# A norm's sum of squares: seven of eight blocks added on GpSimd, two products on TensorE

## The chip, the cores and the metric
One core of a Trainium2 chip runs the whole kernel. The metric is the device time in microseconds, the median of three runs: 1757.07 us before (1756.89 to 1757.11).

## The reference, cut to what matters
A decoder trunk of two layers for 288 tokens (256 of a prompt, 32 of eight samples) of width 1024, in float32. The part that the change touches is the norm, which is computed five times:

```python
def rms_norm(x, g):
    y = xf * lax.rsqrt(jnp.mean(xf * xf, axis=-1, keepdims=True) + RMS_EPS)
    return (y * g).astype(x.dtype)
for layer in range(2):
    h = rms_norm(x, g_norm1[layer]) * (1 + scale1) + shift1     # norms 0 and 2
    ...                                                         # input projection, mixer, output projection
    x = x + gate1 * (concat(o_a, o_b) @ w_out[layer])
    h = rms_norm(x, g_norm2[layer]) * (1 + scale2) + shift2     # norms 1 and 3
    f = swiglu(h, ...) if layer == 0 else moe_swiglu(h, ...)    # dense, then 8 experts
    x = x + gate2 * f
return rms_norm(x, g_final)                                     # norm 4
```

The weights are 1 MB units (w_ada for scale, shift and gate; w_in; w_out; the feed-forward weights), of which some 486 MB are read, most of it in the experts' stage.

## The kernel before, in words
Activations lie channel-major: x is 128 partitions by eight blocks of 288 tokens (`x3[:, d]`, d from 0 to 7; `KD` is 8, `T` is 288). So the mean over channels is a sum over partitions and blocks. A norm n does it in three steps. ScalarE squares block after block as soon as x is ready (`squares`, line 718), into `sqx[n]`, and counts `sq_ready`. TensorE multiplies each block by a matrix of ones and adds up the eight products in one PSUM bank (`norm` of the tensor program, lines 1749 to 1757); a product of two float32 operands is two weight loads and two matmul instructions. ScalarE then makes rstd of it by a logarithm and an exponential (lines 710 and 711), and VectorE forms h (`hf`).

Every engine runs its own program in order, and they wait for each other by semaphores. SP loads the 1 MB units into a ring of six raw buffers; a load waits until the unit six places before it has been used. What lies around the norms:

- Norms 1 and 3 stand behind the output projection. TensorE's products (line 1894) are made into x block by block by three VectorE instructions each (`add_gated`, lines 1453, 1454 and 1458; the last adds two SBUF tensors for the samples). Between them VectorE updates the sample states (line 1436), four heads in two halves. GpSimd writes each head's state out when its second half is done (`gdns_out`, line 665).
- Behind norm 1 TensorE runs four pairs of conditioning products (`ada_run`, line 1722, with short products of line 1732 between them), each from two 1 MB units, and then the dense layer. Behind norm 3 come the router and the experts.
- Norm 2 stands behind the down projection, of whose eight blocks one is ready every 8 us or so; behind it TensorE runs four pairs of conditioning products and then the input projection of layer 1. GpSimd meanwhile waits for x of the last block, clears two pads (line 626), loads their sample rows by DMA (lines 628 and 629), and later forms products for a convolution (line 641).
- Norm 0 works on the input, norm 4 on the result. GpSimd's other arithmetic is the masks of a triangular inverse (line 618).

Of the kernel before, what the change touches and what calls it, by code (L numbers as in the profile page):

```python
# [26 lines left out]
F32 = mybir.dt.float32  # L27
# [3 lines left out]
ALU = mybir.AluOpType  # L31
# [5 lines left out]
KD = D // P  # L37
# [3 lines left out]
T = TP + TS  # L41
# [8 lines left out]
NE = 8  # L50
# [111 lines left out]


SCATTER_AT = range(1, 17, 2)
GATED_AT = range(18, 34, 2)
# [101 lines left out]
def program(nc, units, x_in, c_in, par_in, const_in, gdn_in, qst_in, cst_in,  # L267
            y_out, gdnp_out, gdns_out, qst_out, cst_out):
    ctx = ExitStack()
    with ctx:  # L270
# [24 lines left out]
        sg = keep("sg", 2 * T)  # L295
# [102 lines left out]
        def cc(name, rows=P, cols=None):  # L398
            a, b = CCOL[name]
            return con[0:rows, a:(b if cols is None else a + cols)]  # L400

        def kt(t, n=KD):
            return t[:, :].rearrange("p (k t) -> p k t", k=n)
# [8 lines left out]
        def per_token(m9):  # L412
# [18 lines left out]
        cs_ready, cstat_ready, expa_ready = sem("cs_ready"), sem("cstat_ready"), sem("expa_ready")  # L431
        row_ready, modT_ready, mod_ready = sem("row_ready"), sem("modT_ready"), sem("mod_ready")
        x_ready, sq_ready, ss_ready, rstd_ready = sem("x_ready"), sem("sq_ready"), sem("ss_ready"), sem("rstd_ready")
        hf_ready, hhi_ready, hlo_ready = sem("hf_ready"), sem("hhi_ready"), sem("hlo_ready")
        pad_ready, ab_done, ab_copied, conv_done = sem("pad_ready"), sem("ab_done"), sem("ab_copied"), sem("conv_done")
        silu_done = sem("silu_done")
        low_ready = sem("low_ready")
        posm_ready, parts_ready = sem("posm_ready"), sem("parts_ready")
        router_ready, parts_done, parts_copied = sem("router_ready"), sem("parts_done"), sem("parts_copied")
        moe_added = sem("moe_added")  # L440
# [27 lines left out]
            sem(n) for n in ("tokT_done", "tok_hi_ready", "tok_lo_ready", "lg_done", "lsub_ready", "lexp_ready"))  # L468
        sel_ready, pos_done, npass_ready, posT_ready = (
            sem(n) for n in ("sel_ready", "pos_done", "npass_ready", "posT_ready"))  # L470
        psel_ready, gx_done, gx_copied, gt_done, gw_done, hthi_ready, htlo_ready, ptsel_ready = (
# [135 lines left out]
        def _(pool):  # L607
# [3 lines left out]
            def level_mask(l, b, blk_i, n, q, s):  # L611
# [6 lines left out]
                pool.tensor_tensor(heads(blk[b]["MT"], n, n), heads(blk[b]["AT"], n, n), mask, ALU.mult).then_inc(mt_ready, 1)  # L618

            pool.wait_ge(par_loaded, 16)  # L620
            pool.wait_ge(masks_loaded, 16)
            for l in range(DEPTH):
                if l:
                    pool.wait_ge(st_out, 64 * l)
                    pool.wait_ge(x_ready, 2 * KD * l)
# [37 lines left out]
                for h in range(H):  # L663
                    pool.wait_ge(sst_ready, H * l + h + 1)
                    pool.dma_start(gdns_out[l, h], sst[h][:, :]).then_inc(st_out, 16)

            pool.wait_ge(hf_ready, 8)
# [393 lines left out]
        def _(dve):  # L1061
# [444 lines left out]
            d = 0  # L1506
# [19 lines left out]
            dve.wait_ge(parts_done, 1)  # L1526
            dve.tensor_copy(sg[:, 0:T], ps[:, 7, 0:T]).then_inc(parts_copied, 1)
            dve.wait_ge(lg_done, 1)
# [23 lines left out]
            step(dve.tensor_tensor(sel, o1, o2, ALU.add))  # L1552
            dve.tensor_scalar(sel[:, 2 * NE:3 * NE], sel[:, 2 * NE:3 * NE], cc("valid"), None, ALU.mult).then_inc(sel_ready, 1)
            step(dve.tensor_tensor(g3(o1), g3(o1), wide(m1), ALU.mult))
# [19 lines left out]
            dve.wait_ge(pos_done, 1)  # L1574
            dve.wait_ge(sel_ready, 1)
            step(dve.scalar_tensor_tensor(posm[:, 0:3 * NE], ps[:, 6, 0:3 * NE], 1000.0, sel, ALU.add, ALU.mult))
            dve.tensor_scalar(posm, posm, -1000.0, None, ALU.add).then_inc(posm_ready, 1)
            dve.wait_ge(posm_ready, 1)
            step(dve.tensor_copy(posm[TS:2 * TS, 2 * NE:3 * NE], posm[0:TS, 2 * NE:3 * NE]))
# [5 lines left out]
            dve.wait_ge(pos_done, 2)  # L1585
            dve.tensor_copy(posT[0:NE, :], ps[0:NE, 7, 0:T]).then_inc(posT_ready, 1)
            dve.wait_ge(posT_ready, 1)
            dve.wait_ge(posm_ready, 1)
            dve.wait_ge(pad_ready, DEPTH + 1)
# [14 lines left out]
            step(dve.tensor_copy(parts[:, :, 0], wgt[:, 0:3 * NE]))  # L1604
            dve.tensor_tensor(parts[:, :, 1], wgt[:, 0:3 * NE], parts[:, :, 0].bitcast(F32), ALU.subtract).then_inc(parts_ready, 1)
            dve.wait_ge(npass_ready, 1)
# [92 lines left out]
        def _(pe):  # L1699
# [48 lines left out]
            def norm(n):  # L1748

                bank = NORM_BANK[n]  # L1750
                if n % 2:
                    bank, use, _ = tiles[(("out", n // 2), 2, 0)]
                    pe.wait_ge(bank_free[bank], use + 1)
                for k in range(KD):
                    pe.wait_ge(sq_ready, KD * n + k + 1)
                    last = mm(ps[:, bank, 0:T], cc("ones"), kt(sqx[n])[:, k], start=(k == 0), stop=(k == KD - 1))
                last.then_inc(ss_ready, 1)
# [388 lines left out]
            pe.wait_ge(rstd_ready, 4)  # L2146
            pe.wait_ge(router_ready, 1)
            router = cstat[:, :].rearrange("p (k c) -> p k c", k=KD)
# [14 lines left out]
            token_part(0, range(4))  # L2163
            pe.wait_ge(parts_copied, 1)
            for b in range(3):
# [6 lines left out]

            pe.wait_ge(sel_ready, 1)
            s8 = lambda b: sel[:, NE * b:NE * b + NE]
# [8 lines left out]
            mm(pos(2, 1), cc("ones"), s8(1), start=False, stop=True).then_inc(pos_done, 1)  # L2183
            pe.wait_ge(posm_ready, 1)
            for b in range(3):
# [6 lines left out]
            def gather(g, e, part, bank=7, first=False):  # L2192
# [10 lines left out]
                if part < 2:  # L2203
                    for i, (tok, b) in enumerate(((tok_hi, 0), (tok_hi, 1), (tok_lo, 0), (tok_lo, 1), (tok_hi, 2))):
                        if first and i > 1:
                            pe.wait_ge(tok_lo_ready, i - 1)
                        last = mm(ps[:, bank, :], pe_sel[:, b * P:(b + 1) * P],  # L2207
                                  tok[:, b * D + part * 512:b * D + (part + 1) * 512], start=(i == 0), stop=(i == 4))
                    last.then_inc(gx_done, 1)
                elif part < 4:  # L2210
                    for d in range(4):
                        c = (4 * (part - 2) + d) * P
                        last = pe.transpose(ps[:, bank, d * P:(d + 1) * P], xe[:, c:c + P], cc("ident"))
                    last.then_inc(gt_done, 1)
                else:
                    if first:
                        pe.wait_ge(parts_ready, 1)
                    for b in range(3):
                        mm(ps[:, 7, 0:2], pe_sel[:, b * P:(b + 1) * P], wgt_parts[:, bass.ds(2 * (e + b * NE), 2)],
                           start=(b == 0), stop=(b == 2))  # L2220
                    mm(ps[:, 7, 8:8 + T], ones_r[:, :], pos_e[:, :], start=True, stop=True).then_inc(gw_done, 1)
# [184 lines left out]
```

## Time and profile before

| | us |
|---|---|
| median of the runs | 1757.07 |
| the profiled execution | 1768.01 |
| its span, first to last instruction | 1766.0 |
| TensorE busy | 1719.7 |
| VectorE busy | 1373.1 |
| ScalarE busy | 1034.9 |
| GpSimd busy | 82.2 |

All times of rows are microseconds from the span's start in one profiled execution. Norm 0 lies near 20, norm 1 near 260, norm 2 near 490, norm 3 near 728 and norm 4 near 1758. PE is TensorE, PEld its weight loads, DVE VectorE, ACT ScalarE, POOL GpSimd, SPq the queue that SP issues loads from. PEclk is the TensorE clock that was granted, as a share of the full one.

### The profile page before, as it was taken

How to read it: one execution, taken by the hardware profiler on the slowest of the kernel's cores; microseconds unless marked ns; L12 is line 12 of the kernel's file. 1: busy time of each engine (PE TensorE's matmuls, PEld its weight loads, DVE VectorE, ACT ScalarE, POOL GpSimd, SP SyncE). 2: the span in 40 equal slices, each digit the busy share in tenths (PEclk: the TensorE clock that was granted, in tenths of full speed). 3: DMA queues.
4: the chain of work that ended last, by engine and by line, in shares of the span. 5: the costliest groups of instructions: out<-in, count | busy, mean ns of one | idle time of the engine just before them, and what ended most of it. 6: DMA issues, size and time to landing. Idle time of an engine off the chain costs nothing.

```text
span 1766.0 us, 25378 instructions
## 1 busy us (share of the span) xinstructions
PE 1719.7 (97%) x9412; PEld 1441.3 (82%) x9412; DVE 1373.1 (78%) x1629; ACT 1034.9 (59%) x991; POOL 82.2 (5%) x97
## 2 busy tenths in 40 slices
PE   6999999999999999799999999999999999999997
PEld 3878978999978698578888888888888888888886
DVE  2799365544339974778898898998888988988998
ACT  3345424443334543167777777777777777777775
POOL 0122100000011130100000000000000000000000
PEclk9999899999989998889999999999999999999999
DMA  9875047444477510368999999999999999999996
GB/s 384 333 298 189 25 173 286 167 166 167 144 282 286 193 45 31 120 263 347 360 363 344 359 355 353 355 369 351 365 351 351 361 360 357 368 340 367 362 355 269
DMA packets 73386, 499.49 MB, mean 283 GB/s; under 512 B 8097, under 2 KB 8225, under 8 KB 15297
## 3 DMA queue, kind: packets, MB, share of 16 engines
q1 hardware_dynamic: 69728, 481.17, 71.8%
q0 software_dynamic: 3552, 16.87, 2.5%
q8 instruction: 71, 1.16, 0.3%
q14 instruction: 35, 0.28, 0.0%
HBM read 485.96 MB, written 12.05 MB: 282 GB/s over the span
## 4 chain that ended last, share of the span: by engine, by line
PE 90%; DVE 7%; DMA 2%; issue 1%; ACT 0%; SPq 0%; DVEq 0%
PE ps L2263 17%; PE ps L2264 17%; PE ps L2265 17%; PE ps L1711 5%; PE ps L1712 5%; PE ps L1713 5%; PE ps L2065 4%; PE ps L1894 3%; DVE yc L1136 2%; DMA raw<-units 2%; PE ps L1722 2%; PE ps L2240 1%; PE ps L2207 1%; PE ps L1802 1%; PE ps L1817 1%; PE ps L1815 1%
## 5 line engine op out<-in xcount | busy, mean ns | idle before, releaser
L1066 DVE TENSOR_TENSOR wlo<-raw,whi 128x2048 fp32r<-128x2048 f32 x384 | 877.0, 2292 | 175.4 <-ACT whi L689 175.4
L689 ACT ACTIVATE whi<-raw 128x2048 fp32r<-128x2048 f32 x384 | 735.7, 1918 | 257.5 <-PE ps L2265 203.3
L2263 PE MATMUL ps<-whi,ht_hi 128*128 128x512 f32 x896 | 355.5, 397 | 1.6 <-DVE ht_lo L1615 1.6
L2265 PE MATMUL ps<-whi,ht_lo 128*128 128x512 f32 x896 | 349.4, 390 | 0.0
L2264 PE MATMUL ps<-wlo,ht_hi 128*128 128x512 f32 x896 | 349.3, 390 | 0.0
L2265 PEld LDWEIGHTS ps<-whi,ht_lo 128*128 128x128 f32 x896 | 168.2, 188 | 35.8
L2263 PEld LDWEIGHTS ps<-whi,ht_hi 128*128 128x128 f32 x896 | 168.3, 188 | 34.9 <-issue 1.9
L2264 PEld LDWEIGHTS ps<-wlo,ht_hi 128*128 128x128 f32 x896 | 168.5, 188 | 31.5
L2263 PE MATMUL ps<-whi,at_hi 128*128 128x512 f32 x448 | 175.2, 391 | 0.0
L2265 PE MATMUL ps<-whi,at_lo 128*128 128x512 f32 x448 | 174.4, 389 | 0.0
L2264 PE MATMUL ps<-wlo,at_hi 128*128 128x512 f32 x448 | 174.4, 389 | 0.0
L1711 PE MATMUL ps<-h_hi,whi 128*128 128x288 f32 x560 | 168.0, 300 | 0.0
L1712 PE MATMUL ps<-h_lo,whi 128*128 128x288 f32 x560 | 165.8, 296 | 0.0
L1713 PE MATMUL ps<-h_hi,wlo 128*128 128x288 f32 x560 | 165.2, 295 | 0.0
L1711 PEld LDWEIGHTS ps<-h_hi,whi 128*128 128x128 f32 x560 | 105.5, 188 | 8.5 <-issue 8.4
L1136 DVE SCALAR_TENSOR_TENSOR yc<-cpad,par,yc 128x256 f32<-128x256 f32 x240 | 106.4, 514 | 0.0
L1713 PEld LDWEIGHTS ps<-h_hi,wlo 128*128 128x128 f32 x560 | 106.0, 189 | 0.0
L1712 PEld LDWEIGHTS ps<-h_lo,whi 128*128 128x128 f32 x560 | 105.7, 189 | 0.1
L2265 PEld LDWEIGHTS ps<-whi,at_lo 128*128 128x128 f32 x448 | 84.1, 188 | 17.7
L2263 PEld LDWEIGHTS ps<-whi,at_hi 128*128 128x128 f32 x448 | 84.1, 188 | 16.7
L2264 PEld LDWEIGHTS ps<-wlo,at_hi 128*128 128x128 f32 x448 | 84.1, 188 | 16.6
L2065 PE MATMUL ps<-hf,raw 128*128 128x288 f32 x352 | 93.6, 427 | 2.8 <-DVE hf L1116 2.8
(351 smaller groups left out, 2012.2 us busy)
## 6 DMA issues: line engine op xcount, KB each, us to landing
raw<-units SPq DMA_DIRECT2D x447, 1024.0 KB, 6.3
raw<-units SPq DMA_DIRECT2D x16, 512.0 KB, 5.6
sst<-gdn_in POOLq DMA_DIRECT2D x8, 512.0 KB, 6.8
gdns_out<-sst POOLq DMA_DIRECT2D x8, 512.0 KB, 4.2
qst_out<-qpad POOLq DMA_DIRECT2D x2, 1890.0 KB, 10.8
cst_out<-cpad POOLq DMA_DIRECT2D x2, 1116.0 KB, 13.1
x<-x_in SPq DMA_DIRECT2D x1, 1152.0 KB, 9.0
y_out<-hf SPq DMA_DIRECT2D x2, 576.0 KB, 2.9
```

The lines of the kernel that those rows point to most:

```text
L689: act.activation(whi[s % NSPLIT][:, :], raw[u % NRAW][:, :], ACT.Copy).then_inc(hi_split, 1)
L1066: dve.tensor_tensor(wlo[s % NSPLIT][:, :], raw[unit_of(s) % NRAW][:, :], whi[s % NSPLIT][:, :].bitcast(F32), ALU.subtract).then_inc(lo_spl ...
L1136: dve.scalar_tensor_tensor(y, cp3[:, c, j:j + TP], w, y, ALU.mult, ALU.add).then_inc(tap_prompt, 1)
L1711: mm(out, w_hi, x_hi, start=start, stop=False)
L1712: mm(out, w_hi, x_lo, start=False, stop=False)
L1713: return mm(out, w_lo, x_hi, start=False, stop=stop)
L1722: last = mm(ps[32 * k:32 * k + 32, bank, :], cst3[:, 4 * half + k], raw[u % NRAW][:, k * 512:(k + 1) * 512], start=(half == 0), stop=(half ...
L1894: last = mm(ps[:, bank, 0:T], raw[u % NRAW][:, w], part, start=(k == 0), stop=(k == 3))
L2065: last = mm(ps[:, bank, 0:T], raw[u % NRAW][:, w], hf3[:, k], start=(k == 0), stop=(k == KD - 1))
L2263: mm(ps[:, bank, :], a_hi[:, a], whi[u % NSPLIT][:, w], start=(first and i == 0), stop=False)
L2264: mm(ps[:, bank, :], a_hi[:, a], wlo[u % NSPLIT][:, w], start=False, stop=False)
L2265: last = mm(ps[:, bank, :], a_lo[:, a], whi[u % NSPLIT][:, w], start=False, stop=(end and i == 3))
```

## The change: GpSimd adds seven blocks, TensorE multiplies two
In norms 1, 2 and 3 GpSimd adds blocks 1 to 6 of the squares to block 0, in place, each add behind the square that it takes and behind the add before it. TensorE multiplies block 0 (which by then holds seven blocks) and block 7 by the ones, in place of all eight. Norms 0 and 4 stay. In GpSimd's program the adds of norms 1 and 3 stand behind the four state stores of their layer, those of norm 2 ahead of the pads of layer 1.

```diff
+SUMMED = KD - 2
 # gpsimd
+            def sum_squares(n):
+                q3 = kt(sqx[n])
+                for d in range(1, KD - 1):
+                    pool.wait_ge(sq_ready, KD * n + d + 1)
+                    if d > 1:
+                        pool.wait_ge(sq_summed, SUMMED * (n - 1) + d - 1)
+                    pool.tensor_tensor(q3[:, 0], q3[:, 0], q3[:, d], ALU.add).then_inc(sq_summed, 1)
             for l in range(DEPTH):
                 if l:
+                    sum_squares(2)
                     pool.wait_ge(st_out, 64 * l)
                     pool.wait_ge(x_ready, 2 * KD * l)
...
                     pool.dma_start(gdns_out[l, h], sst[h][:, :]).then_inc(st_out, 16)
+                sum_squares(2 * l + 1)
 # tensor
-                for k in range(KD):
+                for k in range(KD) if n in (0, 4) else (0, KD - 1):
                     pe.wait_ge(sq_ready, KD * n + k + 1)
+                    if n in (1, 2, 3) and k == 0:
+                        pe.wait_ge(sq_summed, SUMMED * n)
                     last = mm(ps[:, bank, 0:T], cc("ones"), kt(sqx[n])[:, k], start=(k == 0), stop=(k == KD - 1))
```

A semaphore more is needed for `sq_summed`. Six semaphores of the routing part (`sel_ready`, `posm_ready`, `posT_ready`, `parts_ready`, `router_ready`, `parts_copied`) become counts of two, `routed` (1 to 4) and `router_ready` (1 and 2); the waits name the same instructions by count. One wait that stood twice is left out.

## Rows read from the trace of the kernel before

**Rows 1.** The page, part 1: busy time, share and instructions of each engine.
```profile
PE 1719.7 (97%) x9412; PEld 1441.3 (82%) x9412; DVE 1373.1 (78%) x1629; ACT 1034.9 (59%) x991; POOL 82.2 (5%) x97
```

**Rows 2.** The norms' line: durations in ns (min/median/max), first and last start.
```profile
L1756 PE MATMUL ps<-sqx,con x80: 405/406/849, 18.5 to 1758.4; 128*128 128x288 f32 x80
```

**Rows 3.** Timeline, norm 1: start, duration (us), engine, line, operation, idle time before.
```profile
251.58 8.03 PE L1894 MATMUL ps<-oall,raw 128*128 128x288 f32 x32
...
256.22 0.53 POOL L665 DMA_DIRECT2D gdns_out<-sst  x1 [0.50 <-DVE sst L1436]
...
258.54 0.44 ACT L718 ACTIVATE sqx<-x 128x288 f32<-128x288 f32 x1 [0.70 <-DVE x L1458]
...
259.44 4.04 PE L1756 MATMUL ps<-sqx,con 128*128 128x288 f32 x16
...
260.27 0.18 DVE L1458 TENSOR_TENSOR x<-x,small 128x32 f32<-128x32 f32 x1
260.48 0.44 ACT L718 ACTIVATE sqx<-x 128x288 f32<-128x288 f32 x1 [1.50 <-DVE x L1458]
...
263.52 0.50 ACT L710 ACTIVATE rstd<-ps,con 128x288 f32<-128x288 f32 x1 [2.59 <-PE ps L1756]
...
264.05 0.44 ACT L711 ACTIVATE rstd<-rstd 128x288 f32<-128x288 f32 x1
```

**Rows 4.** Chain of waits behind norm 1: start, duration, what.
```profile
265.40 7.19 DMA raw<-units
```

**Rows 5.** Timeline, norm 3.
```profile
722.91 0.53 POOL L665 DMA_DIRECT2D gdns_out<-sst  x1 [0.23 <-issue]
...
723.93 0.53 POOL L665 DMA_DIRECT2D gdns_out<-sst  x1 [0.49 <-DVE sst L1436]
...
727.15 4.04 PE L1756 MATMUL ps<-sqx,con 128*128 128x288 f32 x16
...
728.19 0.44 ACT L718 ACTIVATE sqx<-x 128x288 f32<-128x288 f32 x1 [1.50 <-DVE x L1458]
```

**Rows 6.** Timeline, norm 2 and the conditioning products behind it.
```profile
490.11 4.04 PE L1756 MATMUL ps<-sqx,con 128*128 128x288 f32 x16
...
491.14 0.44 ACT L718 ACTIVATE sqx<-x 128x288 f32<-128x288 f32 x1 [8.35 <-DVE x L1458]
...
495.20 10.55 SPq L570 DMA_DIRECT2D raw<-units  x8
...
503.61 1.78 PE L1722 MATMUL ps<-raw,cstat 128*32 128x512 f32 x8 [1.06 <-DMA raw<-units]
```

**Rows 7.** Timeline of GpSimd, two runs of its two-input instructions.
```profile
47.03 2.60 POOL L641 TENSOR_TENSOR taps_s<-cpad,par 128x248 f32<-128x248 f32 x4 [14.04 <-DVE cpad L1193]
...
160.04 2.14 POOL L618 TENSOR_TENSOR MT<-AT,con 128x512 f32<-128x512 f32 x2 [3.38 <-DVE LT L1283]
```

**Rows 8.** The same two lines: durations in ns (min/median/max).
```profile
L641 POOL TENSOR_TENSOR taps_s<-cpad,par x32: 672/889/2742, 47.0 to 590.0; 128x248 f32<-128x248 f32 x32
...
L618 POOL TENSOR_TENSOR MT<-AT,con x26: 507/1092/1596, 153.6 to 672.0; 128x512 f32<-128x512 f32 x24, 32x128 f32<-32x128 f32 x2
```

**Rows 9.** Timeline of GpSimd while VectorE runs masks of two SBUF inputs.
```profile
622.88 3.02 POOL L618 TENSOR_TENSOR MT<-AT,con 128x512 f32<-128x512 f32 x2 [9.98 <-ACT AT L871]
```

**Rows 10.** Stretches: from:to, length, busy time by engine, PEclk, DMA share, GB/s.
```profile
264.00:264.50 0.50, 0.50 (x12) 0.13 (x4) 0.00 (x0) 0.46 (x2) 0.00 (x0) 1.00 0.00 0
...
275.10:278.50 3.40, 3.40 (x16) 3.40 (x16) 0.65 (x3) 3.19 (x2) 0.00 (x0) 0.50 1.01 429
...
494.85:495.50 0.65, 0.65 (x12) 0.24 (x8) 0.25 (x1) 0.31 (x1) 0.00 (x0) 1.00 1.02 230
...
500.00:503.56 3.56, 2.55 (x24) 1.13 (x16) 1.73 (x6) 0.60 (x1) 0.00 (x0) 1.00 1.00 419
...
734.00:736.00 2.00, 0.26 (x4) 0.19 (x8) 1.97 (x7) 0.00 (x0) 0.00 (x0) 0.98 0.00 0
736.00:738.00 2.00, 0.80 (x8) 0.00 (x0) 1.96 (x5) 0.00 (x0) 0.00 (x0) 0.50 0.00 0
```

More of the change, by code:

```diff
@@ L432, in program @@
         row_ready, modT_ready, mod_ready = sem("row_ready"), sem("modT_ready"), sem("mod_ready")
+        sq_summed = sem("sq_summed")
         x_ready, sq_ready, ss_ready, rstd_ready = sem("x_ready"), sem("sq_ready"), sem("ss_ready"), sem("rstd_ready")
@@ L437, in program @@
         low_ready = sem("low_ready")
-        posm_ready, parts_ready = sem("posm_ready"), sem("parts_ready")
-        router_ready, parts_done, parts_copied = sem("router_ready"), sem("parts_done"), sem("parts_copied")
+        router_ready, parts_done = sem("router_ready"), sem("parts_done")
+        WEIGHTS, LOGIT_PARTS = 1, 2
+        routed = sem("routed")
+        CHOSEN, PLACED, TURNED, WEIGHED = 1, 2, 3, 4
         moe_added = sem("moe_added")
@@ L468, in program @@
             sem(n) for n in ("tokT_done", "tok_hi_ready", "tok_lo_ready", "lg_done", "lsub_ready", "lexp_ready"))
-        sel_ready, pos_done, npass_ready, posT_ready = (
-            sem(n) for n in ("sel_ready", "pos_done", "npass_ready", "posT_ready"))
+        pos_done, npass_ready = sem("pos_done"), sem("npass_ready")
         psel_ready, gx_done, gx_copied, gt_done, gw_done, hthi_ready, htlo_ready, ptsel_ready = (
@@ L1526, in _ @@
             dve.wait_ge(parts_done, 1)
-            dve.tensor_copy(sg[:, 0:T], ps[:, 7, 0:T]).then_inc(parts_copied, 1)
+            dve.tensor_copy(sg[:, 0:T], ps[:, 7, 0:T]).then_inc(router_ready, 1)
             dve.wait_ge(lg_done, 1)
@@ L1552, in _ @@
             step(dve.tensor_tensor(sel, o1, o2, ALU.add))
-            dve.tensor_scalar(sel[:, 2 * NE:3 * NE], sel[:, 2 * NE:3 * NE], cc("valid"), None, ALU.mult).then_inc(sel_ready, 1)
+            dve.tensor_scalar(sel[:, 2 * NE:3 * NE], sel[:, 2 * NE:3 * NE], cc("valid"), None, ALU.mult).then_inc(routed, 1)
             step(dve.tensor_tensor(g3(o1), g3(o1), wide(m1), ALU.mult))
@@ L1574, in _ @@
             dve.wait_ge(pos_done, 1)
-            dve.wait_ge(sel_ready, 1)
+            dve.wait_ge(routed, CHOSEN)
             step(dve.scalar_tensor_tensor(posm[:, 0:3 * NE], ps[:, 6, 0:3 * NE], 1000.0, sel, ALU.add, ALU.mult))
-            dve.tensor_scalar(posm, posm, -1000.0, None, ALU.add).then_inc(posm_ready, 1)
-            dve.wait_ge(posm_ready, 1)
+            dve.tensor_scalar(posm, posm, -1000.0, None, ALU.add).then_inc(routed, 1)
+            dve.wait_ge(routed, PLACED)
             step(dve.tensor_copy(posm[TS:2 * TS, 2 * NE:3 * NE], posm[0:TS, 2 * NE:3 * NE]))
@@ L1585, in _ @@
             dve.wait_ge(pos_done, 2)
-            dve.tensor_copy(posT[0:NE, :], ps[0:NE, 7, 0:T]).then_inc(posT_ready, 1)
-            dve.wait_ge(posT_ready, 1)
-            dve.wait_ge(posm_ready, 1)
+            dve.tensor_copy(posT[0:NE, :], ps[0:NE, 7, 0:T]).then_inc(routed, 1)
+            dve.wait_ge(routed, TURNED)
             dve.wait_ge(pad_ready, DEPTH + 1)
@@ L1604, in _ @@
             step(dve.tensor_copy(parts[:, :, 0], wgt[:, 0:3 * NE]))
-            dve.tensor_tensor(parts[:, :, 1], wgt[:, 0:3 * NE], parts[:, :, 0].bitcast(F32), ALU.subtract).then_inc(parts_ready, 1)
+            dve.tensor_tensor(parts[:, :, 1], wgt[:, 0:3 * NE], parts[:, :, 0].bitcast(F32), ALU.subtract).then_inc(routed, 1)
             dve.wait_ge(npass_ready, 1)
@@ L2146, in _ @@
             pe.wait_ge(rstd_ready, 4)
-            pe.wait_ge(router_ready, 1)
+            pe.wait_ge(router_ready, WEIGHTS)
             router = cstat[:, :].rearrange("p (k c) -> p k c", k=KD)
@@ L2163, in _ @@
             token_part(0, range(4))
-            pe.wait_ge(parts_copied, 1)
+            pe.wait_ge(router_ready, LOGIT_PARTS)
             for b in range(3):
@@ L2171, in _ @@
                 token_part(b, range(KD)).then_inc(tokT_done, 1)
-            pe.wait_ge(sel_ready, 1)
+            pe.wait_ge(routed, CHOSEN)
             s8 = lambda b: sel[:, NE * b:NE * b + NE]
@@ L2183, in _ @@
             mm(pos(2, 1), cc("ones"), s8(1), start=False, stop=True).then_inc(pos_done, 1)
-            pe.wait_ge(posm_ready, 1)
+            pe.wait_ge(routed, PLACED)
             for b in range(3):
@@ L2216, in gather @@
                     if first:
-                        pe.wait_ge(parts_ready, 1)
+                        pe.wait_ge(routed, WEIGHED)
                     for b in range(3):
```

## The prediction
> **What bounds the kernel now.** I read the page's busy shares first: TensorE is busy 97% of the span, GpSimd 5% [rows 1]. So time taken from TensorE counts, but only where it is TensorE that ends a stage. The row by line for the norms' products shows what is on offer: 80 instructions for five norms of eight blocks, so 16 for a norm and two for a block, the median one 406 ns, at intervals of about 0.24 us [rows 2]. The change takes 12 of the 16 away in three of the norms, at most 12 x 0.242 = 2.9 us in each. Whether it is gained depends on what ends last around each of them, so I then read the timeline of norms 1, 3 and 2.
>
> Norm 1 [rows 3]: the last output product ends at 259.6, the norm's products follow without a gap and end at 259.44 + 4.04 = 263.48. The last square ended at 260.48 + 0.44 = 260.92, so TensorE is what is late, by 2.6 us. Behind it nothing is idle: the chain goes from these products to the first conditioning products, and from 265.40 over a weight transfer that these set off to the next stage [rows 4]. Norm 3 is the same picture: products from 727.15 to 731.19, the last square done at 728.63, then ScalarE's two steps and VectorE [rows 5]. Norm 2 is another: its first seven squares are long done (ScalarE had been idle for 8.35 us when the last began), the last ends at 491.58, the products run from 490.11 to 494.15; but after them TensorE comes to a wait of 1.06 us for a weight transfer, at 503.61 [rows 6].
>
> **The change part by part.** It puts six adds of 128x288 on GpSimd in each of norms 1, 2 and 3, in one chain (each waits for the one before it, and for its square), and TensorE's first product waits for the sixth. Norms 0 and 4 keep eight products.
>
> *One add.* The trace of before has no 128x288 add on GpSimd. Its nearest rows: four of 128x248 in 2.60 us while VectorE does nothing that disturbs them, 0.65 us from one to the next [rows 7]; two of 128x512 in 2.14 us, 1.07 each [rows 7]. That is 0.42 us for 264 elements, 1.6 ns each, so 0.65 + 40 x 0.0016 = 0.71 us. These follow each other without waiting for completion. A chained add also waits for the completion before it: 0.03 us for the part that overlaps now (a single one takes 0.68) and some 0.05 for the semaphore (ScalarE's second step of a norm starts 0.03 us after its first ends [rows 3]). I take 0.79 us a link. Bounds: 0.51, the smallest of line L618's rows, and 1.14, its median of 1.09 (most of them 128x512) with the same wait [rows 8].
>
> The Trainium skill, GPSIMD Engine Reference, section 3.1, measures 2.6 cycles of 1.2 GHz for an element of a two-input add, 2.2 ns, where the rows here give 1.6. By that figure a link would be 0.17 us longer and the six 1.0 us longer; an estimate from that page, which the rows here don't bear out.
>
> *Norm 1.* GpSimd comes to its adds only after the four state stores. The last is issued at 256.22 and takes 0.53 [rows 3]; between two issues of which the second waits for nothing lie 0.23 us [rows 5], so the first add starts at 256.98. Six links are 4.74 us: 261.72. The squares never hold it: the sixth block's ends at 258.54 + 0.44 = 258.98, the last add starts after 260.9. To this comes contention with VectorE: line L1458 (x and small, both in SBUF, 0.18 us) runs three times in that time (the last at 260.27). That such pairs hold each other up is in the trace: with VectorE's 128x512 masks of two SBUF inputs beside them GpSimd's two took 3.02 us in place of 2.14 [rows 7, 9]. Three meetings of 0.18 us are 0.54 at most; I take 0.2: 261.9. The Trainium skill, SBUF — State Buffer, section "Who interferes with whom", states it as a lock: of a VectorE instruction with two SBUF inputs and a GpSimd one that reads SBUF the second waits for the first to finish. By that rule x of block 7 comes late by up to one add, 0.79 us.
>
> That delay, whatever its cause, is hidden: x of block 7 is ready at 260.45 now; 0.8 later its square ends at 261.7, and its product's turn is after block 0's.
>
> TensorE then has two products. By the present spacing they end 0.24 + 3 x 0.242 + 0.41 = 1.38 us after the first weight load, so 261.9 + 0.05 + 1.38 = 263.33, against 263.48: -0.15 us. TensorE's 2.9 us of work are gone, and in their place it waits 2.3 us for GpSimd. Bounds: at 0.51 a link the sum is there at 260.0 and the square of block 7 decides: 260.97 + 0.24 + 0.242 + 0.41 for one product = 261.9, -1.6. At 1.14 with all 0.54: 264.36 + 1.43 = 265.8, +2.3. What comes behind moves one for one: in 264.0 to 264.5 no transfer runs [rows 10], because the next loads wait for the conditioning products behind the norm.
>
> *Norm 3.* The last store ends at 724.46, the first add starts at 724.69, the sum is ready at 729.6, the products end at 731.06 against 731.19: -0.15 us, with the bounds of norm 1. Behind it VectorE and the router's products wait for rstd, with no transfer in the way, so it passes on whole.
>
> *Norm 2.* The sixth add follows the seventh square, which ended at 491.14 - 8.35 = 482.8, seven us ahead of its use: GpSimd hides it at any price of the bounds. It stands there in front of the pads' memset, which waits for x of block 7 anyway (ready before the square of 491.14), so nothing in GpSimd's queue moves. TensorE runs block 0 at once and block 7 from 491.65: end 492.54 in place of 494.15, 1.6 us sooner. The conditioning products start sooner by that, and so do SP's loads, which wait for each of them (first at 495.20 [rows 6]). But from 494.85, where the first packets would then come, to 503.56 the DMA engines' share is 1.0 in the rows at both ends [rows 10] and 0.96 at the least between: they are busy, first with the pads. The same bytes land no sooner, so TensorE still gets its last half at 503.61 and only waits 1.6 us longer. I take 0; bounds -1.6 (if the loads overtake the pads) and +0.1.
>
> *The rest.* Six semaphores become counts of two others. VectorE increments them in the same order as before, each wait asks for the same instruction, and one doubled wait goes: 0. The two waits ahead of TensorE's first product are in the 0.05.
>
> *Sum*: -0.15 + 0 - 0.15 = -0.3 us on the profiled execution's 1768.01 us (span 1766.0 and 2.0 around it), 1767.7. The median of the unprofiled runs, 1757.07, is 10.9 below the profiled one; the stages are the same, so I carry the difference over: 1756.8. The bounds add up to -4.8 and +4.7.
>
> **The rivals.**
> *The sum comes late* (slower). The chain of six adds, not TensorE's spacing, ends norms 1 and 3. It decides from the link at which today's end is met: (263.48 - 1.43 - 0.2 - 256.98) / 6 = 0.81 us; from there each 0.1 us costs 0.6 in either norm. For it: my 0.79 is just under, the median of the disturbed 128x248 adds is 0.889 [rows 8], and at that, 0.97 with the wait, the cost is +0.95 a norm, in all +1.9: 1759.0. At the upper bound of both norms it is +4.6: 1761.7. Against it: only short VectorE instructions run beside these adds. The GPSIMD page's 2.6 cycles lead here too.
> *TensorE's clock falls in the new gap* (slower). After 4.5 us without products from 731.2 the granted clock was 0.50 in 736 to 738, its lower level of 1.2 GHz, and behind the conditioning products and a short wait within them it was 0.50 from 275.1 to 278.5 [rows 5, 10]. The change puts 2.3 us of idle time into norm 1. One such stretch more, 3.4 us at half clock, gives half of it away: +1.7, so 1758.5. Against it: the gap from 731.2 had lasted almost its 4.5 us before the clock fell (0.98 in 734 to 736 [rows 10]), and the new one is half as long; and in norm 3 a fall that comes sooner meets no products but the norm's own two. The Trainium skill, TensorE: Matmul & The Clock Gate, section "Why this matters for your kernels", also warns of idle gaps between bursts of products.
> *The gain passes* (faster). Without waits between links, 0.71 and no meeting, norms 1 and 3 end 0.7 + 0.8 sooner, and norm 2 gives its 1.6, if the loads' own place in the queues and not the engines' work sets their landing: -3.1, so 1754.0. Against it: the DMA share [rows 10] and the chained waits.
> That the change doesn't do what it says can't be seen from here: the adds are on GpSimd and the twelve products are gone by the text.
>
> **How the numbers follow.** Forecast 0.61, within 1755.5 to 1758.0. Sum late 0.14, clock 0.13, gain passes 0.12. The range, from near the third rival to beyond the second and most of the first: 1754.0 to 1760.5. A measurement of this kernel tells about 0.2%, 3.5 us, from no change. Faster than 1753.6 needs the third rival beyond its sum: 0.06. Slower than 1760.6 needs the first near its bound, or both slow ones together: 0.08. Else the same: 0.86.
>
> **What would show it.** 80 instructions of the norms' line become 44; six GpSimd adds of 0.74 us at steps of 0.79 behind the last store, in one run; TensorE idle for 2.3 us ahead of its products in norms 1 and 3, and rstd at the present distance from the last output product; in norm 2 the wait for the transfer at 503.6 grown from 1.06 by 1.6 us. The prediction is wrong if the adds' step is under 0.7 or over 0.9, if norm 2's wait does not grow, or if granted clocks of 0.50 stand where now is 1.00.

## The result: 0.28% slower

The changed kernel took 1763.41 us (median of 7 runs, 1762.11 to 1765.14) against 1757.11 for the kernel before (7 runs, 1754.65 to 1760.17): a ratio of 1.0028, with an interval of 1.0016 to 1.0039. The forecast was 1756.8 with a range to 1760.5. The ratios of this text are those on record; the quotient of two medians can lie 0.1% beside them (here it is 1.0036).

The profiled execution of before was an unusual one: 1768.0 us, longer than all of its timed runs. The changed kernel's own took 1762.1. So the two spans say the reverse of the times, and a whole trace against a whole trace proves nothing here. The unchanged kernel profiled again (the first experiment) had a span of 1759.3 us; it stands for before below, and stages are compared over several traces.

The profile after, its page: span, and busy time by engine [rows 1].

```profile
span 1760.1 us, 25339 instructions
...
PE 1705.8 (97%) x9376; PEld 1427.8 (81%) x9376; DVE 1376.0 (78%) x1629; ACT 1034.9 (59%) x991; POOL 96.6 (5%) x115
```

The norms' line and the new adds, min/median/max in ns:

```profile
L1770 PE MATMUL ps<-sqx,con x44: 405/406/849, 18.5 to 1752.5; 128*128 128x288 f32 x44
```

```profile
L629 POOL TENSOR_TENSOR sqx<-sqx x18: 790/796/822, 253.5 to 722.5; 128x288 f32<-128x288 f32 x18
```

36 matmul instructions are gone and 18 adds have come, as the text says (80 of [rows 2] are 44). TensorE lost 14 us of busy time between the two traces and the kernel is slower all the same.

The timeline of norm 1 after, which answers to [rows 3]; the second number is the duration, or the whole of a run of instructions:

```profile
251.58 4.77 PE L1908 MATMUL ps<-oall,raw 128*128 128x288 f32 x19
...
252.97 0.53 POOL L677 DMA_DIRECT2D gdns_out<-sst  x1 [0.50 <-DVE sst L1449]
253.21 1.17 DVE L1471 TENSOR_TENSOR x<-x,small 128x32 f32<-128x32 f32 x1
253.52 5.49 POOL L629 TENSOR_TENSOR sqx<-sqx 128x288 f32<-128x288 f32 x6
...
254.92 0.39 DVE L1471 TENSOR_TENSOR x<-x,small 128x32 f32<-128x32 f32 x1
...
257.23 0.44 ACT L731 ACTIVATE sqx<-x 128x288 f32<-128x288 f32 x1 [0.50 <-DVE x L1471]
259.15 2.26 PE L1770 MATMUL ps<-sqx,con 128*128 128x288 f32 x4 [2.80 <-POOL sqx L629]
...
261.45 0.50 ACT L723 ACTIVATE rstd<-ps,con 128x288 f32<-128x288 f32 x1 [3.78 <-PE ps L1770]
```

The six adds follow the last store at once and take 5.49 us, (5.49 - 0.79) / 5 = 0.94 from one to the next. TensorE comes free at 256.35, waits 2.80 us for them, and then needs 2.26 us for two products. Their end, 261.41, is 5.06 us behind the last output product; before it was 3.88 [rows 3]. The reason for the 2.26 stands in the stretches (columns as in [rows 10]): most of the gap is still at full clock, and from 258.82 on, 2.5 us behind the end of the last output product, it is the half one, the lower level of 1.2 GHz.

```profile
256.40:258.80 2.40, 0.00 (x0) 0.00 (x0) 0.76 (x3) 0.77 (x2) 2.11 (x3) 1.00 0.60 162
258.82:262.20 3.38, 3.05 (x9) 1.37 (x13) 0.00 (x0) 0.72 (x2) 0.19 (x1) 0.50 0.51 213
...
720.70:723.00 2.30, 0.00 (x0) 0.00 (x0) 0.85 (x4) 0.75 (x2) 2.01 (x3) 1.00 0.63 192
723.10:726.00 2.90, 2.26 (x4) 1.17 (x4) 0.00 (x0) 0.27 (x1) 0.19 (x1) 0.50 0.56 234
```

The last two are norm 3; the clock fell there 2.4 us behind the last output product. [rows 5] had products of 4.04 us right behind the output products, and now there are four instructions after a wait:

```profile
723.43 2.26 PE L1770 MATMUL ps<-sqx,con 128*128 128x288 f32 x4 [2.80 <-POOL sqx L629]
```

Norm 2 after, TensorE's timeline [rows 6]:

```profile
487.75 0.75 PE L1770 MATMUL ps<-sqx,con 128*128 128x288 f32 x2 [0.89 <-ACT sqx L731]
488.43 3.64 PE L1734 MATMUL ps<-raw,cstat 128*32 128x512 f32 x32
...
497.58 1.83 PE L1734 MATMUL ps<-raw,cstat 128*32 128x512 f32 x8 [1.68 <-DMA raw<-units]
500.06 1.58 PE L1734 MATMUL ps<-raw,cstat 128*32 128x512 f32 x8 [0.65 <-DMA raw<-units]
...
503.38 1.46 PE L2079 MATMUL ps<-hf,raw 128*128 128x288 f32 x5
```

The products end 1.75 us sooner behind the last square than in [rows 6]; 1.6 was forecast. The two last halves of the conditioning units are both waited for, and the input projection starts 15.7 us behind the last square; in the control it was 15.3, in the trace of [rows 6] 17.2. The clock fell here too, at 497.75, 0.17 us behind the first of the two waits:

```profile
497.70:501.20 3.50, 2.85 (x16) 0.24 (x14) 0.00 (x0) 0.00 (x0) 0.00 (x0) 0.51 1.02 424
```

This table is worked out from all the traces: the length of three stages in us, in brackets how much of it ran at half clock. The first goes from the last output product of layer 0 to the first product of the dense layer, the second from the last down product to the first input product of layer 1, the third from the last output product of layer 1 to the experts' first.

```
norms 1,3 / norm 2        kernel             norm 1       norm 2       norm 3
eight / eight             e1_before          15.2 (0.0)   16.6 (1.3)   34.8 (20.5)
eight / eight             e4_names           15.1 (0.0)   16.4 (0.9)   34.4 (20.5)
eight / two               e2_norm2           15.1 (0.0)   18.5 (6.5)   33.6 (20.5)
two / eight               e3_norms13         16.6 (3.4)   16.6 (0.0)   35.6 (27.3)
two / two (changed)       first trace        16.7 (3.4)   17.0 (3.4)   35.5 (27.3)
two / two (changed)       f1_after           16.6 (3.4)   17.3 (3.4)   35.6 (27.3)
two, filled / two         f2_filled          15.3 (0.0)   19.4 (6.2)   33.7 (20.5)
two, early / two          g3_early           14.1 (0.0)   19.0 (6.2)   32.4 (20.5)
five / eight              f3_three           18.5 (6.3)   16.4 (0.0)   32.8 (20.5)
four / eight              f4_four            13.9 (0.0)   19.0 (4.8)   32.3 (23.9)
four / eight              g4_four_again      14.1 (0.0)   16.6 (0.0)   32.7 (20.5)
eight / eight, late pads  g2_padslate_eight  15.0 (0.0)   15.0 (0.0)   34.5 (20.5)
eight / two, late pads    g1_padslate_sum2   15.1 (0.0)   15.1 (0.0)   34.4 (20.5)
four / eight, late pads   h1_best            14.4 (0.0)   15.3 (0.0)   32.3 (23.9)
```

Of the stages that are left, the one between norms 1 and 2 is 213.3 us in all but two of the traces, and the input projection and mixer of layer 1 scatter from 214 to 221 us whatever the kernel, with 10 to 24 us at half clock. That scatter is why single traces can't be summed.

The table also shows a third place. Norm 2 with the sum and the pads loaded early stands in five of its rows, and in all five the clock fell 10.1 to 11.9 us behind the last square, right behind the first of the waits for the last two halves or within the second (2.3 to 3.5 us of waiting in all). With eight products and early pads there are seven traces, that of before among them: one wait of 0.9 to 1.4 us, and in two of the seven a fall ahead of the last conditioning product's end. The last half landed 11.9 to 12.7 us behind the last square with the sum and 11.8 to 12.6 with eight, though its load was issued 1.75 us sooner. The stage is 18.2 us long on average with the sum (17.0 to 19.4) and 17.2 with eight (16.4 to 19.0, with 18.5 for the trace of before). These ranges overlap, so the clock's fall is seen in every trace with the sum, and what it costs is not settled.

### The profile page after: what moved, and what is told of

The parts are those of the page before. It is cut to its first block, busy times and chain, and to the rows that moved or that the text cites. A ratio compares the mean times of both kernels' runs of the same rounds, so it can differ in the third digit from the quotient of the medians.

```text
span 1760.1 us, 25339 instructions
## 1 busy us (share of the span) xinstructions
PE 1705.8 (97%) x9376; PEld 1427.8 (81%) x9376; DVE 1376.0 (78%) x1629; ACT 1034.9 (59%) x991; POOL 96.6 (5%) x115
## 4 chain that ended last, share of the span: by engine, by line
PE 64%; DVE 6%; issue 1%; DMA 1%; ACT 0%; POOL 0%; DVEq 0%; POOLq 0%
PE ps L2277 17%; PE ps L2279 17%; PE ps L2278 17%; DVE yc L1149 2%; PE ps L2254 1%; PE ps L2079 1%; PE ps L1908 1%; PE ps L2221 1%; DVE wlo L1079 1%; DMA raw<-units 1%; PE ps L1816 1%; PE ps L1831 1%; PE ps L1829 1%; DVE conv L1169 1%; PE ps L2239 0%
## 6 DMA issues: line engine op xcount, KB each, us to landing
cst_out<-cpad POOLq DMA_DIRECT2D x2, 1116.0 KB, 12.6
```

## The experiments

Ratios are of the kernel to the kernel before, timed on the same chip, with their 95% intervals.

**The control.** No edit.

> The kernel before, unchanged, as a control. The measured result was 1763.4 against 1757.1 us, while the two profiled executions said the reverse: 1768.0 before, 1762.1 after. Theory A (the stages of the norms make the difference): the profiled execution of before was an unusual one; this one shows a span near 1755 us, and norm 1 and 3 end 1.2 us sooner behind their last output product than in the changed kernel (3.9 against 5.1 us). Theory B (executions scatter by some us whatever the kernel, by transfers and clock): the time differs from the kernel before by 2 us or more though nothing is changed.

Measured: 1758.39 us (11 runs, 1755.05 to 1761.14) against 1758.78 (35 runs), ratio 0.9989 (0.9979 to 0.9998). Theory A's point on the profile held in the main: the norms of this trace end 3.88 us behind the last output product, and its span is 1759.3, not 1766, though 1755 was expected. Theory B's difference of 2 us did not come (the medians are 0.4 us apart), but it has its part: executions of one kernel scatter by 6 us and more, and a comparison of a kernel with itself came out 0.11% off, with an interval that leaves out 1. What follows is read with that in mind: of a ratio alone nothing of about 0.1% is a finding, whatever its interval.

**Norm 2 alone; norms 1 and 3 alone; neither.** The edit is a number of adds for each norm (`ADDS`), from which TensorE's products follow; the three are {1: 0, 2: 6, 3: 0}, {1: 6, 2: 0, 3: 6} and all 0.

```diff
-SUMMED = KD - 2
+ADDS = {1: 0, 2: 6, 3: 0}
...
-                for d in range(1, KD - 1):
+                for d in range(1, ADDS[n] + 1):
...
-                for k in range(KD) if n in (0, 4) else (0, KD - 1):
+                for k in [0, *range(ADDS.get(n, 0) + 1, KD)]:
```

> The changed kernel with GpSimd's sum in norm 2 alone; norms 1 and 3 have eight products on TensorE again. Theory A (the late sum of norms 1 and 3 costs; norm 2 gains what its trace shows, 1.5 us up to the first input product): 1755.5, 1.5 below before. Rival B (the cost lies behind norm 2, where loads now start 1.7 us sooner among the pads): slower than before, 1760 to 1763. Rival C (the six semaphores made counts of two cost it): also 1762.

Measured: 1759.83 us, ratio 1.0009 (1.0001 to 1.0018). Not 1.5 us faster as Theory A had it: the gain at norm 2 does not arrive. B's price of 1760 to 1763 is missed by 0.2 us at its lower end, and the kernel without any sum (below) has the same ratio, so the time alone does not tell whether norm 2 costs anything.

> The changed kernel with GpSimd's sum in norms 1 and 3 alone; norm 2 has eight products on TensorE again. Theory A (the sum comes 1.2 us late in each, and TensorE's clock falls in the gap): 2.4 us for the late sums and 1.7 to 5 for the clock, 1761 to 1764. Rival B (norm 2 costs): 1759.5, 2.4 above before and no more.

Measured: 1760.32 us, ratio 1.0017 (1.0005 to 1.003), between the prices of A (1761 to 1764) and B (1759.5). The half clock stands in the gap of norm 1 and of norm 3 again, and the products end 5.07 and 5.06 us behind the last output product. By the stages the larger part of the loss is here; beside the kernel without any sum, 1759.75 on the same chip, the times alone don't show it.

> The changed kernel without any sum on GpSimd: five norms of eight products, only the routing's six semaphores are counts of two. Theories A and B: as before, 1757 within 1 us. Rival C (the semaphores cost it): 1762 or so.

Measured: 1759.75 us, ratio 1.0009 (0.9995 to 1.0022). The merged semaphores can't be told from nothing, and the stages of its trace are those of the control. The interval alone would still allow 3.9 us; against rival C speaks also `g2_padslate_eight` below, which has the same merged semaphores and eight products everywhere, at 0.9994 (0.9984 to 1.0003).

**The changed kernel again, and with the gap filled.**

> The changed kernel, unchanged, beside the three below. In its first trace the two products of norm 1 ended 5.06 us behind the last output product, against 3.88 before, and a stretch at half clock began in the gap ahead of them (at 258.8); the same in norm 3 (from 723.0). Theory A (the gap lets TensorE's clock fall; without that the two products would end 3.9 us behind the last output product, as before): 1.2 us lost in either norm and up to 0.5 on the conditioning products, 1761 to 1763, and the half clock stands in the gap again in both norms. Rival B (the first comparison was 2 to 4 us off by scatter between executions): 1759 to 1760.

Measured: 1763.08 us (12 runs) against 1758.62 (35 runs), ratio 1.0027 (1.0013 to 1.004), on another chip than the experiments above. The first result stands, and so does the fall of the clock, from 259.4 in norm 1 and from 727.0 in norm 3. The edit for the filled gap:

```diff
+                for k in range(1, 6) if n in (1, 3) else ():
+                    pe.wait_ge(sq_ready, KD * n + k + 1)
+                    mm(ps[:, bank, 0:T], cc("ones"), kt(sqx[n])[:, k], start=True, stop=True)
                 for k in range(KD) if n in (0, 4) else (0, KD - 1):
```

> The changed kernel; in norms 1 and 3 TensorE also forms the products of blocks 1 to 5 while it waits for GpSimd's sum. They go to the norm's bank, which the product of block 0 then overwrites, so nothing but TensorE's idle time changes. Theory A (the clock falls by the idle gap): no half clock at norm 1, the norm's last product 3.9 to 4.1 us behind the last output product, 2.2 us gained in all against the changed kernel. Rival B (the sum's lateness itself costs the 1.2 us): still 5.0 us behind.

Measured: 1760.48 us, ratio 1.0005 (0.9993 to 1.0017), 2.6 us under the changed kernel on the same chip (12 runs from 1757.99 to 1762.07, against 12 from 1760.07 to 1768.10). The adds come as late as before; only TensorE's idle time is gone. Norm 1 of its timeline, then two stretches:

```profile
254.22 5.49 POOL L629 TENSOR_TENSOR sqx<-sqx 128x288 f32<-128x288 f32 x6
...
256.89 2.59 PE L1768 MATMUL ps<-sqx,con 128*128 128x288 f32 x10
...
259.86 1.21 PE L1773 MATMUL ps<-sqx,con 128*128 128x288 f32 x4 [0.38 <-POOL sqx L629]
```

```profile
257.10:259.30 2.20, 2.20 (x10) 1.52 (x8) 0.76 (x3) 0.77 (x2) 1.91 (x3) 1.00 0.51 134
259.30:262.70 3.40, 3.02 (x21) 1.23 (x24) 0.53 (x1) 0.94 (x2) 0.41 (x1) 1.00 0.58 241
```

The two products take 1.21 us, not 2.26, and end 4.02 us behind the last output product, not 5.06. So of the 1.18 us that either norm lost, 1.04 are the clock's, and 0.14 the lateness of the sum. Work that is thrown away made the changed kernel faster.

**Fewer adds.** Three adds are {1: 3, 2: 0, 3: 3} in the edit above. Four have an order of their own:

```diff
+                ORDER = {1: [5, 6, 0, 7], 3: [5, 6, 0, 7]}
+                blocks = ORDER.get(n, [0, *range(ADDS.get(n, 0) + 1, KD)])
+                for k in blocks:
```

> GpSimd adds three blocks to block 0 in norms 1 and 3 (at 0.94 us a link the sum is there just as TensorE comes free), TensorE forms five products; norm 2 has eight on TensorE. Theory A: no gap, no fall, the last product 2.85 us behind the last output product against 3.88 before: 1.0 gained in either norm, 1756.8 where before is 1758.8. Rival B (fewer products let the clock fall all the same, or behind them time is given back): no faster than before.

Measured: 1763.05 us, ratio 1.0019 (1.0005 to 1.0033). The products end 2.66 us behind the last output product, better than forecast, and the time is worse than before. In its trace the clock fell for 10.2 us from 271.9, behind norm 1, so that the stage took 18.5 us. One trace can't say how often that comes: the profiled execution of before had such a stretch at 275.1 [rows 10], the control had none. Theory A is right on the norm and wrong on the time. A part that does show is 1.6 us given back at the experts (below), but the next kernel gives that back too; why this one did worse is open.

> GpSimd adds four blocks in norms 1 and 3; TensorE forms the products of blocks 5, 6, the sum and 7, in this order, so the sum has 1 us more; norm 2 has eight on TensorE. Theory A: 2.4 us behind the last output product, 1.5 gained in either norm, 1755.8 where before is 1758.8; it lies at the square of block 7 (its end plus 0.9), the least this norm can take. Rival B: as in the run with three.

Measured: 1760.03 us, ratio 0.9994 (0.998 to 1.0008).

> The run with four adds in norms 1 and 3 and the order 5, 6, sum, 7 again, to narrow its time (0.9994, interval 0.998 to 1.0008). Theory A: 1.7 us gained in either norm by its trace, 1755.5 to 1757.5 where before is 1758.7. Rival (what the clock does later takes it back): 1758.7 or more.

Measured: 1756.25 us against 1759.67, ratio 0.999 (0.9978 to 1.0001), on a third chip. There is no gap, and the products end 2.16 us behind the last output product (2.4 was expected), which is 0.84 us behind the last square:

```profile
254.21 3.63 POOL L630 TENSOR_TENSOR sqx<-sqx 128x288 f32<-128x288 f32 x4
...
256.88 2.32 PE L1773 MATMUL ps<-sqx,con 128*128 128x288 f32 x8
...
257.93 0.44 ACT L732 ACTIVATE sqx<-x 128x288 f32<-128x288 f32 x1 [0.50 <-DVE x L1472]
```

Both norms gain 1.7 us, 3.4 in all, and the two ratios show 1.1 and 1.8 us, each with an interval that includes no gain. A part of the rest shows in the stretches around the experts' first products (at 747.7 in this kernel, at 752.0 in the one with eight), this kernel's first:

```profile
744.70:748.00 3.30, 1.65 (x12) 1.38 (x13) 1.75 (x4) 2.89 (x4) 0.00 (x0) 1.00 0.48 204
748.10:751.50 3.40, 3.40 (x10) 2.64 (x9) 2.29 (x1) 0.41 (x1) 0.00 (x0) 0.50 0.00 0
```

The same of `e4_names`:

```profile
749.70:753.00 3.30, 1.65 (x10) 1.29 (x9) 1.88 (x5) 2.89 (x3) 0.00 (x0) 1.00 0.28 114
753.00:760.00 7.00, 7.00 (x33) 5.79 (x33) 4.48 (x2) 4.87 (x4) 0.00 (x0) 1.00 0.41 151
```

Either has a stretch at full clock around its first products; in this kernel a half one follows. The first 24 product instructions of the experts took 7.45 us here and 5.84 there. It was so in all four traces with three or four adds (7.40 to 7.45) and in none of the eleven others, that of before among them (5.81 to 5.86): 1.6 us given back. An earlier start is not enough for it: in `g3_early` (next) the experts start 32.4 us behind the last output product, as soon as in these four (32.3 to 32.8), and are not hit. What goes with it in all 15 traces is the time since the clock last rose: the experts' first product came 3.0 to 3.1 us behind that in the four, and 2.2 to 2.5 or 3.7 us in the others. That this is the cause is not shown; no run shifted the experts' products alone.

**The first three adds ahead of the stores.**

```diff
+                sum_squares(2 * l + 1, 1, 4)
                 for h in range(H):
                     pool.wait_ge(sst_ready, H * l + h + 1)
                     pool.dma_start(gdns_out[l, h], sst[h][:, :]).then_inc(st_out, 16)
-                sum_squares(2 * l + 1)
+                sum_squares(2 * l + 1, 4, KD - 1)
```

> The changed kernel, but in norms 1 and 3 GpSimd's first three adds stand ahead of the four state stores, the other three behind them; two products on TensorE. The sum is there 2.8 us sooner, so TensorE's gap is 1.3 us and ends with the last square. Theory A (the loss comes of the late sum and the clock's fall in a gap of 2.7 us): the last product 2.2 to 2.4 us behind the last output product, no half clock in front of it, 1759 to 1760 (the cost of norm 2 stays). Rival B (two products and any gap let the clock fall): products of 0.48 us spacing as in the changed kernel, 1762.

Measured: 1759.8 us, ratio 1.0005 (0.9994 to 1.0015). GpSimd and TensorE in norm 1:

```profile
247.42 1.76 POOL L629 TENSOR_TENSOR sqx<-sqx 128x288 f32<-128x288 f32 x2 [4.43 <-ACT sqx L732]
...
253.00 1.75 POOL L629 TENSOR_TENSOR sqx<-sqx 128x288 f32<-128x288 f32 x2 [0.45 <-ACT sqx L732]
```

```profile
256.29 1.24 PE L1771 MATMUL ps<-sqx,con 128*128 128x288 f32 x4 [0.89 <-POOL sqx L629]
```

Two products, six adds, a gap of 0.89 us in place of 2.80, and no fall of the clock: they end 2.13 us behind the last output product, 2.9 sooner than in the changed kernel; in norm 3 it is the same. So neither the two products nor GpSimd beside VectorE is what cost; the length of the gap is. (Both norms gain 1.75 us and the time shows none of it. The stage of norm 2, 19.0 us, took most of it back in this trace, with 6.2 us at half clock.)

**The pads held back.** This asks why norm 2 gives nothing. GpSimd issues the pads' loads of layer 1 only when TensorE has used the sixth half, in the kernel with the sum in norm 2 alone and in the one with none.

```diff
                 pool.memset(cp3[:, :, 0:CK - 1], 0.0).then_inc(pad_ready, 1)
+                if l:
+                    pool.wait_ge(ada_used, ADA_AT[LANDS["ada", *ADA_NORM[2][2][:1], 2 * ADA_NORM[2][2][1] + 1]] + 1)
```

> GpSimd's sum in norm 2 alone, and the pads' loads of layer 1 held back until TensorE has used the sixth half of the conditioning units behind norm 2, so that the weights go first. Theory A (in norm 2 the gain is lost because the DMA engines are busy with the pads when the loads come 1.75 us sooner): now the last half's products end 1.7 us sooner behind the last square than in the run with eight products and late pads, and both end sooner than with early pads (12.9 us). Rival B (the loads take their time whatever runs beside them, since the four outstanding ones share the engines): they end less than 0.7 us sooner than in that run.

Measured: 1758.69 us, ratio 0.9997 (0.9985 to 1.0008).

> All norms with eight products on TensorE, the pads' loads of layer 1 held back as in the run above. Both theories: TensorE's wait of 0.9 us for the last half goes, its products end 12.0 us behind the last square of norm 2 in place of 12.9. Time: 1757 to 1759, as before or 1 us less, unless VectorE then waits for the pads.

Measured: 1757.47 us, ratio 0.9994 (0.9984 to 1.0003). The last halves, with the sum in norm 2 (last square ended at 488.64):

```profile
496.78 1.06 PE L1737 MATMUL ps<-raw,cstat 128*32 128x512 f32 x8
499.17 1.06 PE L1737 MATMUL ps<-raw,cstat 128*32 128x512 f32 x8 [1.33 <-DMA raw<-units]
```

and with eight products (last square ended at 486.88):

```profile
496.78 2.04 PE L1737 MATMUL ps<-raw,cstat 128*32 128x512 f32 x16
```

With eight, the wait of 0.88 us for the last half is gone, and the input projection starts 13.7 us behind the last square in place of 15.1: the pads did stand in the way. But with the sum TensorE still waits, 1.33 us, and its last half ends only 0.34 us sooner behind the last square than with eight (11.60 against 11.94), and the input projection starts at 13.7 us in either. That is rival B: the loads start 1.75 us sooner and hardly land sooner. Why they take longer from issue to landing is not shown. The forecast of no gain at norm 2 was right; of its reason, transfers that are busy first with the pads, the pads are one part, since without them in front the gain does not come either.

**Both gains together.**

> Four adds on GpSimd in norms 1 and 3 with the products in the order 5, 6, sum, 7; norm 2 with eight products; the pads' loads of layer 1 held back until the sixth conditioning half has been used. Theory: the two gains add up, 1.7 us each in norms 1 and 3 and 1.3 us at norm 2 (the input projection began 13.7 us behind its last square in place of 15.1): 4 us in all, ratio 0.9975 to 0.9985. Rival: as in the run with four adds alone, 0.999, because the scatter of the clock in the mixer takes the rest.

Measured: 1758.91 us (12 runs, 1751.15 to 1762.83) against 1758.06 (17 runs), ratio 0.9991 (0.9974 to 1.0007). The theory's 0.9975 to 0.9985 did not come; the rival's 0.999 did. The three stages of the norms add up to 62.0 us, the least of all traces (14.4, 15.3, 32.3), but the mixer of layer 1 took 218.6 us with 17.1 at half clock, and the experts' start 1.6 more. No version was shown to beat the kernel before; this one and that of four adds stand 0.06% to 0.1% under it, and the intervals of both include 1.

## Why the prediction was wrong, step by step

- *What bounds each norm* (norms 1 and 3 by TensorE's eight products, norm 2 by the transfer behind it): right. With an earlier sum the norm does gain 1.7 us.
- *One add*: 0.74 us forecast, 0.796 measured; *a link*: 0.79 forecast, 0.94 measured. The larger error is the wait on the add before: I gave it 0.05 us behind that add's end, after ScalarE's step of 0.03 us; on GpSimd it is 0.145. *The start* behind the last store: 0.23 forecast, 0.02 measured. So the six adds took 5.49 us in place of 4.74, and the start and the 0.2 for contention, which did not come, take 0.4 off again. TensorE's first product followed the sum at 0.14 us in place of 0.05 and started 2.8 us behind the last output product, where 2.35 was forecast. (The aside with 0.17 us more a link comes to 0.96, near the 0.94, but by an add of 0.91, which is 0.796: the two errors in it cancel.)
- *Contention with VectorE*: it is there (x's last step took 1.17, 0.39 and 0.40 us in place of 0.18), it hit VectorE and not the adds, and it was hidden, as forecast.
- *The end of norms 1 and 3*: -0.15 us forecast. The link's error makes it +0.14, shown by the filled gap. That alone would have left the time where it was. The rival *The sum comes late* had its condition met (0.94 over 0.81 a link), but by its own price that would be 0.8 us a norm; it was 0.29 more than forecast.
- *The clock.* The step that failed is the choice against the rival "TensorE's clock falls in the new gap". I had the gap at 2.3 us, weighed it against one of 4.5 us in the same trace, and took half as long for short enough; chance 0.13. At 2.8 us it fell in both norms of all three traces that have the gap, each time 2.4 to 2.5 us behind the last output product; whether a gap of the forecast length would have brought it no run shows. I also bounded it wrongly in norm 3: I wrote that the fall meets no products there but the norm's own two, and just these two cost 1.04 us. Price of it: 1.04 in norm 3, 1.04 and some 0.3 on the conditioning products in norm 1.
- *Norm 2*: 0 forecast. The 1.6 us do come (1.75) and are lost, as forecast. It is not quite 0: the stage was 17.0 and 17.3 us in the two traces of the changed kernel (17.0 to 19.4 in all five with the sum and early pads) and 16.4 to 16.6 in five of the seven with eight products there and early pads (18.5 and 19.0 in the others, with more at half clock). With the sum TensorE reaches its waits sooner and waits longer, and in all five traces the clock fell there, in front of the last products. The forecast saw the longer wait and did not price the clock in it, though the rival on the clock was on the table.
- *The semaphores*: 0 forecast, nothing shown.
- *The sum.* The stages give +1.5, +0.6 and +0.9 us, 3.0 in all or 0.17% (3.5 with norm 2 by the averages of all traces); the two timed comparisons say 0.28% and 0.27%, 4.9 and 4.7 us, with lower bounds of 0.16% and 0.13%. The two halves of the change gave 0.17% and 0.09% by themselves, and the kernel with neither 0.09%. Some 2.4 us of the 3.0 are the clock's in the two gaps. Between 3.0 and 4.9 us something may be left; the mean granted clock was 0.979 over the runs of the changed kernel and 0.982 to 0.983 over those of before, so it is likely more of the same in stages that scatter, but no run shows where.
- *The range* ended at 1760.5, 0.2% up. It left out the adds' upper bound in both norms (1761.7), and the clock's fall was in it once, where it came in both gaps and at norm 2.
- *The signs.* Two of the three signs of being wrong came: the adds' step was over 0.9, and granted clocks of 0.50 stand where 1.00 was. The third did not, since the wait at norm 2 grew (1.68 and 0.65 in place of 1.06).

## What to carry to other kernels

Work taken from TensorE is worth nothing where something else must first arrive, and it costs where the time that is freed becomes a gap ahead of TensorE's next products: compare the gap with the shortest one in the trace behind which the clock fell, not the longest, and price it in every place at once, a wait for a transfer that grows longer among them. Split such a sum so that the helper's part is ready when TensorE comes free, and let TensorE do the blocks that remain (four adds and four products here, where each norm gained 1.7 us, though the whole kernel was not shown to be faster). Chains of short adds on GpSimd pay for their wait at every link, so they should start as early as their first input, ahead of queued stores.

## What the runs showed of the hardware

- A GpSimd add that waits for the completion of the one before it follows it at 0.94 us where it takes 0.796; those without such a wait followed at less than their duration (0.65 us from one to the next, 0.672 the shortest single one [rows 7, 8]).
- Idle gaps of 2.80 us ahead of TensorE's next product brought the half clock each time (six of six, in three traces, 2.4 to 2.5 us behind the last product); gaps of 0.89 us (`g3_early`) and 0.38 us (`f2_filled`) in the same place did not (two of two each). The Trainium skill, TensorE: Matmul & The Clock Gate, section "Why this matters for your kernels", advises against idle gaps between bursts of products. The gaps of 2.80 us bear the advice out, though the ones that it names are longer than these; there the measurement decides.
- Waits for transfers amid TensorE's products, two of them with 2.3 to 3.5 us in all, went with a fall of the clock in five of five traces; with one of 0.9 to 1.4 us it fell ahead of the last conditioning product's end in two of seven.
- Two SBUF inputs on VectorE beside GpSimd: an instruction of 0.18 us took up to 1.17, and the three slowed ones of norm 1 each ended 0.05 to 0.06 us behind the end of one of GpSimd's adds, which kept to 0.79 to 0.82 us. That agrees with the lock that the Trainium skill, SBUF — State Buffer, section "Who interferes with whom", describes. The longest one is recorded as starting 0.31 us ahead of the add, so which engine has to wait doesn't follow from the recorded starts.
- Loads that are issued 1.75 us sooner behind the last square, with others behind them in flight: the second of them landed 0.3 us sooner (the first 0.7) with nothing of the pads in their way, one trace against one, and no sooner with the pads in front (11.9 to 12.7 us in five traces, 11.8 to 12.6 in seven).
